# Stick-breaking attention: two products per unit and running sums of later key blocks on VectorE

## The reference, cut to what matters

```
z        = (q @ k.T) * scale                     # [512 queries, 512 keys], per head
valid    = key < query
log_keep = where(valid, log_sigmoid(-z), 0)
log_tail = cumsum of log_keep from the last key down, minus log_keep
w        = where(valid, exp(log_sigmoid(z) + log_tail), 0)
out      = w @ v
```

## Time and profile before

| | |
|---|---|
| median of 3 runs | 2872.91 us (2870.44 to 2874.6) |
| profiled execution, its own time | 2878.19 us |
| its span, first to last instruction | 2876.4 us |
| TensorE busy | 2628.1 us, 91% of the span |
| VectorE, ScalarE busy | 1089.8 us (38%), 708.5 us (25%) |
| mean granted TensorE clock | 0.962 of full speed |
| the stick-breaking stage | 45.85 us in each of the two layers |

### The profile page before, as it was taken

One profiled execution on the slowest core, in us unless ns is written; L12 is line 12 of the kernel. 1 busy time (PEld: TensorE's weight loads), 2 busy tenths in 40 slices (PEclk: granted clock), 3 DMA queues, 4 the chain that ended last, 5 costly groups with the idle time before them and its releaser, 6 DMA issues. The chain is left out here.

```text
span 2876.4 us, 43155 instructions
## 1 busy us (share of the span) xinstructions
PE 2628.1 (91%) x17316; PEld 1391.2 (48%) x17316; DVE 1089.8 (38%) x2320; ACT 708.5 (25%) x1851; POOL 219.5 (8%) x256
## 2 busy tenths in 40 slices
PE   7999999999998899998799999987899969999987
PEld 3565654664645666655344444435566543332222
DVE  3022340213345665457322121236652562333224
ACT  2134321333322245332111111113342321000000
POOL 1100200000101001012000000001100010000000
PEclk9999999999999999998899999998999979999999
DMA  7244615442614001115899999972102239999996
GB/s 224 82 128 106 166 55 139 110 132 78 158 50 118 6 1 43 66 47 212 321 392 395 401 401 395 400 216 54 28 1 95 96 143 358 410 406 410 411 410 262
DMA packets 268621, 569.96 MB, mean 198 GB/s; under 512 B 12416, under 2 KB 203200, under 8 KB 219328
## 3 DMA queue, kind: packets, MB, share of 16 engines
q1 hardware_dynamic: 256512, 528.69, 50.3%
q0 software_dynamic: 11824, 39.18, 5.0%
q10 hardware_dynamic: 144, 0.14, 0.0%
HBM read 551.53 MB, written 16.42 MB: 197 GB/s over the span
## 5 line engine op out<-in xcount | busy, mean ns | idle before, releaser
L460 PE MATMUL ps<-turned,ring 128*128 128x512 f32 (+1 forms) x1408 | 551.3, 552 | 10.2 <-ACT turned L1594 8.8
L460 PEld LDWEIGHTS ps<-turned,ring 128*128 128x128 f32 x1408 | 270.6, 193 | 279.6 <-issue 259.0
L705 PE MATMUL ps<-ring,mixT 128*128 128x512 f32 x512 | 224.1, 597 | 0.8 <-DVE mixT L1775 0.8
L1249 ACT ACTIVATE work<-ps 128x512 f32<-128x512 f32 x32 | 19.1, 598 | 684.5 <-PE ps L1153 404.3
L506 PE MATMUL ps<-kz,qz 96*128 96x256 f32 (+3 forms) x384 | 165.6, 519 | 24.0 <-DVE qz L2197 8.8
L705 PEld LDWEIGHTS ps<-ring,mixT 128*128 128x128 f32 x512 | 97.0, 191 | 118.7 <-issue 117.3
L1816 ACT ACTIVATE probsT<-ps 128x512 f32<-128x512 f32 (+3 forms) x280 | 120.2, 455 | 136.4 <-PE ps L546 106.7
L1803 ACT ACTIVATE probs_v<-ps,col 128x256 f32<-128x256 f32 (+5 forms) x216 | 136.4, 632 | 70.2 <-DVE col L1753 35.0
L1749 DVE TENSOR_REDUCE col<-ps 128x1 f32<-128x256 f32 (+4 forms) x136 | 78.8, 579 | 176.0 <-PE ps L506 169.6
L471 PE MATMUL ps<-ring,turned 128*128 128x128 f32 x1216 | 140.3, 278 | 4.5 <-ACT turned L1594 4.5
L532 PE MATMUL ps<-const,probs_v 128*128 128x128 f32 x752 | 125.6, 284 | 20.2 <-DVE probs_v L1767 18.1
(11 more groups left out here) (299 smaller groups left out, 3575.4 us busy)
## 6 DMA issues: line engine op xcount, KB each, us to landing
ring<-in_w_gate SPq DMA_DIRECT2D x64, 1024.0 KB, 20.0
mixT<-in_w_up SPq DMA_DIRECT2D x64, 1024.0 KB, 13.9
ring<-in_w_mod SPq DMA_DIRECT2D x96, 512.0 KB, 4.0
ring<-in_w_up SPq DMA_DIRECT2D x48, 1024.0 KB
ring<-in_w_in SPq DMA_DIRECT2D x82, 512.0 KB, 7.3
turned<-in_w_gate SPq DMA_DIRECT2D x32, 1024.0 KB
mixcT<-in_w_down SPq DMA_DIRECT2D x32, 1024.0 KB
probs_v<-in_w_down SPq DMA_DIRECT2D x32, 1024.0 KB
```

Of the source, the lines that this page charges most:

```text
L460: mm = nc.tensor.matmul(ps[:, b, 0:n], w[:, k, :], rhs[:, k, 0:n], start=(k == 0), stop=(k == KD - 1))
L705: mm = nc.tensor.matmul(ps[:, b, :], lhs[:, k, tl * P:(tl + 1) * P], w, start=(k == 0), stop=(k == KD - 1))
```

## The change

Units B and C, after their own products have been made, get the softplus of the unit behind them added to their own part in place, on VectorE: C's part behind its own diagonal then holds the sum over B and A, and B's the sum over B and A at the last queries. So step 4 of a unit is two products at most: its own block with the triangle, and the part of the unit behind it, which is by then a sum over all later blocks, with the matrix of -1. The second product of C waits for B's sum, and that of D for C's sum (`sb_summed`). On VectorE the sum of unit n - 2 stands behind step 3 of unit n and ahead of step 6 of unit n - 2, and it waits for unit n - 2's own products, which read what it overwrites.

```diff
@@ pe_stick
-                    for j in range(i, 4):
-                        if j == i:
-                            pe.wait_ge(*at("softplus", (l, m)))
-                        mm = nc.tensor.matmul(ps[:, m % 4, (j - i) * P:w], cst(C_TRI if j == i else C_NEG1),
-                                              sp[:, hh % 2, sp_off[j]:sp_off[j] + SEQ - j * P], start=False,
-                                              stop=True, skip_group_check=True)
+                    pe.wait_ge(*at("softplus", (l, m)))
+                    mm = nc.tensor.matmul(ps[:, m % 4, 0:w], cst(C_TRI), sp[:, hh % 2, sp_off[i]:sp_off[i] + w],
+                                          start=False, stop=True, skip_group_check=True)
+                    if i < 3:
+
+                        if i < 2:
+                            pe.wait_ge(*at("sb_summed", (l, m - 1)))
+                        mm = nc.tensor.matmul(ps[:, m % 4, P:w], cst(C_NEG1), sp[:, hh % 2, sp_off[i + 1]:sp_off[i + 1] + w - P],
+                                              start=False, stop=True, skip_group_check=True)
                     mm.then_inc(*done("sb_logw", (l, m)))
@@ dve_stick
+            def add_behind(n):
+                hh, i = sb_unit(n)
+                if i in (1, 2):
+
+                    dve.wait_ge(*at("sb_logw", (l, n)))
+                    if i == 1:
+                        dve.wait_ge(*at("sb_summed", (l, n - 1)))
+                    mine = sp[:, hh % 2, sp_off[i] + P:sp_off[i] + SEQ - i * P]
+                    later = sp[:, hh % 2, sp_off[i + 1]:sp_off[i + 1] + SEQ - (i + 1) * P]
+                    nc.vector.tensor_tensor(mine, mine, later, ALU.add).then_inc(*done("sb_summed", (l, n)))
+
...
                 if 2 <= n < 4 * HEADS + 2:
+                    add_behind(n - 2)
                     weights(n - 2)
```

## The result

The changed kernel takes 2926.01 us (median of 5 runs, 2916.18 to 2927.38) against 2872.91 (5 runs, 2870.44 to 2879.82). The ratio is 1.0163, 95% interval 1.0144 to 1.0182. The forecast was 2871.3 us in a range of 2867 to 2876.5, so it was wrong, and by far. The medians are 53.1 us apart and the profiled executions 38.0: the profiled one of the changed kernel is the fastest of its five, and that of the kernel before took 5.3 us more than its median. What follows accounts for the profiled pair.

A forecast was written before the change was run, and what follows sets the result against it. TensorE mostly bounds the stage, with waits on ScalarE and VectorE. Of 6.9 us work removed, C's wait leaves 0.8 us gain per layer, 1.6 in all: 2872.91 becomes 2871.3 us, range 2867 to 2876.5.

The forecast's parts named there:

- the stage's gain passes on as a shift: Behind the stage: TensorE's own projection and the expert transfers just start earlier, so the 1.6 us gain carries through.
- the 48 instructions are simply not issued: In the stage: the 48 removed MATMUL instructions, 6.9 us of work, are gone, so the change surely does what it says.
- Within the stage the sum: Gains of the four heads, 0, 0.21, 0.22 and 0.37 us, make 0.8 us per layer, 1.6 us for both.
- its bounds: Limits on the change's effect on the time, from the cost of VectorE's sum and TensorE's restart: -3.1 to +1.8 us.
- two of its signs: Wrong if D's second product waits, the stage's clock is below 1.00, or idle before C's is much under 0.4 us.
- C's second product waits for B's sum: Ahead of C's second product, TensorE waits 0.4 to 1.2 us for VectorE's sum, 8 times.
- the row of before: On VectorE, the instruction behind D's triangle multiply started 0.20 us after it, before the multiply's 0.29 us were over.
- The rule that the prediction took from the Trainium skill: On VectorE: each sum would start 0.09 us later, making the gain 0.9 us instead of 1.6; not adopted.
- The rival that the clock falls: In heads two and three: one fall costs 6.8 us, giving 2878.1 us; one in each layer gives 2884.9; chance 0.05.
- A clock below 1.00 in the stage: Inside the stage: a granted TensorE clock under 1.00 would show the prediction wrong.
- that no single wait grows beyond about 1.2 us: TensorE's waits in the stage: none grows beyond about 1.2 us, argued against a fall of the clock.
- The rival that TensorE's queue is what counts: In the stage: all 6.9 us of removed TensorE work is gained, giving 2866.0 us; chance 0.06.

The follow-up runs named there:

- the two by two: Four kernels: with the change, loop at slot 0 (2875.99 us) or 200 (2924.17 us); the kernel before, slot 0 (2882.84 us) or 200 (2922.18 us).
- after_pad24: Changed kernel plus 24 extra 128-wide float32 products (96 instructions) at the head of TensorE's program, no alignment directive: 2883.11 us, ratio 1.0028.

## Why the prediction was wrong, step by step

The step that failed is the sentence that the stage's gain passes on as a shift, which puts the effect on all that follows at nothing. With it goes the sentence that excludes any surprise because the 48 instructions are simply not issued: they are not issued, and that is what moved the loop. I followed data, semaphores and transfers of weights behind the stage, and never asked where the code stands. Taking 96 instructions out of straight code ahead of a loop of 1614 moved the loop from a place where it stays on the engine to one where it is loaded at each of 5 back edges: 45.7 us in the expert stretch of the profile, 38 to 45 us in the badly placed kernels of the two by two. No rival had it. The four corners of that table, the 8 slots between 176 and 184, and after_pad24 show it; it isn't an inference from the trace alone.

Within the stage the sum held, and its bounds and two of its signs did not. Timeline of the changed kernel, second head of layer 0, for the earlier trace rows:

```profile
227.22 0.81 PE L585 MATMUL ps<-work,const 128*128 128x384 f32 x2
...
228.47 0.29 DVE L2006 TENSOR_TENSOR work<-work,const 128x128 f32<-128x128 f32 x1
228.68 0.28 DVE L2018 TENSOR_TENSOR work<-work 128x128 f32<-128x128 f32 x1
...
229.02 0.70 PE L591 MATMUL ps<-work,const 128*128 128x256 f32 x2 [0.99 <-DVE work L2018]
229.76 0.43 DVE L2018 TENSOR_TENSOR work<-work 128x256 f32<-128x256 f32 x1
229.99 1.02 PE L585 MATMUL ps<-work,const 128*128 128x512 f32 x2
230.85 0.81 PE L591 MATMUL ps<-work,const 128*128 128x384 f32 x2
```

- C's second product waits for B's sum: 0.99 us here, 1.76 in the first head, 1.06 in the third, 0.23 in the fourth. The prediction named 0.4 to 1.2 for all eight, so it missed the first head on one side and the fourth on the other; the first head's is longer, since the transpose that used to stand in that time now stands behind it.
- The sum starts 0.21 us behind the strict triangle (228.47 to 228.68) and not 0.29: so the row of before was right. The rule that the prediction took from the Trainium skill (VectorE: DVE Perf Modes, The DRAIN you can't avoid), that the next instruction starts when the pipeline is empty, does not hold for these two; the section itself adds that an instruction which isn't held starts earlier.
- The sums take 0.28 and 0.43 us (0.29 and 0.42 foreseen). D's products take 230.85 + 0.81 - 229.99 = 1.67 us (1.68), and D waits for nothing.
- TensorE is busy for 36.39 us (36.4), and an undisturbed stage is 44.92 us (45.0 to 45.1). The gain of 0.93 is 0.13 above the sum. Head by head in layer 1, by where D's products end, it is 0.10, 0.22, 0.22 and 0.39 us; the prediction had 0, 0.21, 0.22 and 0.37.

The rival that the clock falls has to be raised from a 5% side case to a common one: 10 of 16 stages had at least one fall, worth 1.7 to 5.1 us, and none of six before. A clock below 1.00 in the stage was named as a sign of being wrong, and it came in layer 0 (0.96). On the average of the 16 it takes the 0.93 us back and about 1 us more. Its place, heads two and three, was right for 13 of the 17 falls. I had priced it at 6.8 us from a longer fall; here one costs 1.7 at the least. The reason given against it, that no single wait grows beyond about 1.2 us, was wrong: the first head's is 1.76.

The rival that TensorE's queue is what counts was wrong for this form of the change and nearly right for the other: the same 3.4 us of work taken out of a layer's stage brought 0.93 us with C's wait and 2.78 without it.

## What to carry to other kernels

A change of straight code moves every loop behind it. Where a loop's body is large (here 1614 instructions), compare the instruction packets of the two pages and look for waits on issue at the loop's head before anything else is explained; fix the loop's slot, or hint its back edge, before small changes are compared, and look for a wait on issue at the loop's entry as well (2.1 to 3.6 us in three of the kernels here). When sums move from TensorE to VectorE, write them so that no product waits for a later unit: the work taken out was the same, the worth of it three times as much.

## What was not expected of the hardware

- TensorE's loop of 1614 instructions ran 43 us faster over 5 back edges when its first instruction stood at slot 176 of 256 instead of 184 (expert stretch 500.5 against 543.5 us, 97 against 142 instruction packets, one execution each). In the changed kernel each back edge costs 9 us: 4.7 and 1.5 us of standing still, and a slower pace between and behind them.
- With a branch hint the same body at slot 200 was loaded no more often than at slot 0 (97 packets).
- TensorE's clock fell to the 1.2 GHz level (granted clock 0.50) in 10 of 16 stages whose longest wait is 1.76 us, each time within 1.4 us of the end of one of C's waits. It held at 2.4 GHz in the other 6, in 4 stages with the same work and no wait over 1.17 us, and in 2 with C's waits filled. What spared the 6 is open.
